# A gated-convolution and gMLP decoder with grouped experts on one core: the beginning of the expert stages, four more early loads, and stationary tiles of 128 columns

## The reference

```python
x = layer_norm(ALPHA * x + mixer(x), ...)
scores = sigmoid(x @ router_w)            # 16 experts in 4 groups
# the best group by the sum of its two best, and in it the two best experts per token
gates = scores of the two, divided by their sum
for e in range(16):
    h = silu(x @ w_gate[e]) * (x @ w_up[e])      # 1024 -> 512
    y = y + gates[:, e:e+1] * (h @ w_down[e])    # 512 -> 1024
x = layer_norm(ALPHA * x + y, ...)
```

## Time and profile before

| | |
|---|---|
| median of three runs | 1124.26 us |
| the profiled execution | 1123.61 us, its span 1122.0 us |
| PE busy | 1103.2 us, 98% |
| DVE busy | 827.8 us, 74% |
| ACT busy | 652.2 us, 58% |
| POOL busy | 115.2 us, 10% |
| first expert stage | from about 208 to 497 us |
| second expert stage | from about 811 to 1100 us |

### The profile page before, as it was taken

One profiled execution on the slowest core, in us unless ns is written; L12 is line 12 of the kernel. 1 busy time (PEld: TensorE's weight loads), 2 busy tenths in 40 slices (PEclk: granted clock), 3 DMA queues, 4 the chain that ended last, 5 costly groups with the idle time before them and its releaser, 6 DMA issues.

```text
span 1122.0 us, 15395 instructions
## 1 busy us (share of the span) xinstructions
PE 1103.2 (98%) x5448; PEld 872.4 (78%) x5448; DVE 827.8 (74%) x1023; ACT 652.2 (58%) x761; POOL 115.2 (10%) x104
## 2 busy tenths in 40 slices
PE   9999999899999999999999999999999999999996
PEld 8888888577777777777888888888757777777774
DVE  4554546899888989989516545535699898988996
ACT  4422323588887888854417332213558788887873
POOL 2000000031111111021000000000004111111113
PEclk9999999999999999999999999999999999999999
DMA  9925421699999999988304222340389999999986
GB/s 333 401 80 222 150 94 40 224 394 392 390 374 394 385 389 378 395 270 310 144 25 162 101 75 76 137 164 38 114 335 376 407 378 395 378 387 388 386 296 175
DMA packets 51752, 295.97 MB, mean 264 GB/s; under 512 B 8932, under 2 KB 9092, under 8 KB 22128
## 3 DMA queue, kind: packets, MB, share of 16 engines
q1 hardware_dynamic: 36096, 252.46, 58.1%
q0 software_dynamic: 9040, 20.91, 6.4%
q10 hardware_dynamic: 6560, 21.87, 5.1%
HBM read 277.07 MB, written 29.62 MB: 273 GB/s over the span
## 4 chain that ended last, share of the span: by engine, by line
PE 96%; DVE 2%; ACT 1%; issue 1%; DMA 0%; DVEq 0%; SPq 0%; ACTq 0%
PE ps L482 28%; PE ps L484 28%; PE ps L483 28%; PE ps L2050 2%; PE ps L1967 2%; PE ps L1892 1%; PE ps L2190 1%; PE ps L1874 1%; PE ps L1992 1%; PE ps L2090 1%; PE ps L1863 1%; PE ps L2103 0%; DMA raw<-in_w_dense 0%; DVE lo L478 0%; PE ps L1915 0%
## 5 line engine op out<-in xcount | busy, mean ns | idle before, releaser
L478 DVE TENSOR_TENSOR lo<-raw,hi 128x1024 fp32r<-128x1024 f32 x320 | 376.8, 1220 | 87.8 <-ACT hi L467 86.7
L467 ACT ACTIVATE hi<-raw 128x1024 fp32r<-128x1024 f32 x320 | 323.5, 1056 | 116.2 <-PE ps L484 80.2
L482 PE MATMUL ps<-hi,xgT_hi 128*112 128x512 f32 x480 | 190.3, 396 | 0.0
L484 PE MATMUL ps<-hi,xgT_lo 128*112 128x512 f32 x480 | 188.7, 393 | 0.0
L483 PE MATMUL ps<-lo,xgT_hi 128*112 128x512 f32 x480 | 187.5, 391 | 0.0
L478 DVE TENSOR_TENSOR lo<-raw_more,hi 128x1024 fp32r<-128x1024 f32 x128 | 153.5, 1222 | 30.1 <-ACT hi L467 27.9
L467 ACT ACTIVATE hi<-raw_more 128x1024 fp32r<-128x1024 f32 x128 | 132.9, 1057 | 53.6 <-DMA raw_more<-in_w_moe 38.9
L482 PE MATMUL ps<-xT_hi,hi 128*128 128x512 f32 x320 | 126.5, 395 | 0.8 <-DVE lo L478 0.8
L483 PE MATMUL ps<-xT_lo,hi 128*128 128x512 f32 x320 | 124.6, 389 | 0.0
L484 PE MATMUL ps<-xT_hi,lo 128*128 128x512 f32 x320 | 124.6, 389 | 0.0
L484 PEld LDWEIGHTS ps<-hi,xgT_lo 128*112 128x112 f32 x480 | 83.8, 175 | 26.1
(11 more groups left out here) (217 smaller groups left out, 1474.8 us busy)
## 6 DMA issues: line engine op xcount, KB each, us to landing
raw<-in_w_moe SPq DMA_DIRECT2D x128, 1024.0 KB
raw_more<-in_w_moe SPq DMA_DIRECT2D x64, 1024.0 KB
raw<-in_w_dense SPq DMA_DIRECT2D x39, 1024.0 KB
y_rows<-X ACTq DMA_DIRECT2D x4, 2048.0 KB, 25.5
X<-y_rows POOLq DMA_DIRECT2D x10, 512.0 KB, 9.3
x_rows<-X ACTq DMA_DIRECT2D x8, 512.0 KB, 2.6
Y<-y_rows SPq DMA_DIRECT2D x6, 512.0 KB, 5.5
xT_raw<-in_x_t SPq DMA_DIRECT2D x4, 512.0 KB, 6.3
```

The lines of the kernel that those rows point to most:

```text
L467: nc.scalar.activation(hi[:, s, :], flat(raw_units(n)), ACT.Copy).then_inc(hi_ready, 1)
L478: eng.tensor_tensor(lo[:, s, :], flat(raw_units(n)), hi[:, s, :], ALU.subtract).then_inc(lo_ready, 1)
L482: nc.tensor.matmul(out_, a_hi, b_hi, start=first, stop=False)
L484: return nc.tensor.matmul(out_, a_lo, b_hi, start=False, stop=last)
```

## The change

It has these parts:

1. **More early loads.** Units 12 to 15 of each expert stage are loaded raw into the place in `lo` in which their own `lo` part will stand (`raw_lo`); `split_lo` then works in place. Their loads wait only for the end of the mixer's last matmuls. From unit 16 on, the 12 raw slots are used as before.
2. **Expert 0 starts on half of x0.** `first_rows` signals after its first four blocks, ACT copies them then, and `gate_up_first` waits for DVE's half only at its fifth unit.
3. **Expert 0 writes banks 2 and 3.** gate_up(1) does not wait for `hid` of expert 0 any more, turn_h(0) moves behind the first unit of gate_up(1) and `turned_hot` behind its seventh. The counts and the first row numbers now share bank 7, so `route_most` moves ahead of hidden(0) and the routing matmuls wait for it.
4. **ACT's order.** All four late splits of expert 1 stand ahead of x_hi(1). The copy to `hotT` stands in turn(0) behind its fourth split. The load of the norm's parameters `ffn_par` moves behind the loop.
5. **128 columns.** POOL zeroes columns 112 to 127 of `xgT_hi`, `xgT_lo`, `hT_hi`, `hT_lo` at the beginning of each expert stage, and the passes of `gate_up` and `down` for experts 0 to 14 take all 128 columns. `down_last` stays at 112.
6. Two semaphores are dropped and others used in their place.

```diff
+AHEAD = 4
+FIRST = len(RAW_ORDER) + AHEAD
+RAW_SLOTS = RING + MORE + AHEAD
 def raw_slot(n):
-    return slot_of(n) if layer_of(n) is None else RAW_ORDER[(n - MOE[layer_of(n)]) % len(RAW_ORDER)]
+    if layer_of(n) is None:
+        return slot_of(n)
+    j = n - MOE[layer_of(n)]
+    if len(RAW_ORDER) <= j < FIRST:
+        return RING + MORE + j - len(RAW_ORDER)
+    return RAW_ORDER[(j if j < FIRST else j - FIRST) % len(RAW_ORDER)]
...
+        raw_lo = place("raw_lo", [P, RING, UN], F32)
+        lo = nc.alloc_sbuf_tensor_at("lo", [P, RING, UN], F32R, offset=top[0] - RING * UN * 4)
...
-                if raw_slot(n) >= RING and n - MOE[layer_of(n)] < len(RAW_ORDER):
+                if raw_slot(n) >= RING and n - MOE[layer_of(n)] < FIRST:
                     sp.wait_ge(unit_used, MOE[layer_of(n)])
... POOL, experts
+                for side in (xgT_hi, xgT_lo, hT_hi, hT_lo):
+                    chain.post(nc.gpsimd.memset(side[:, :, T:P].bitcast(F32), 0.0))
                 chain.step(nc.gpsimd.tensor_copy(ident_b[layer][:, :], ident[:, :]))
... ACT, turn
                     for k in range(GU - 1):
+                        if is_zero(e) and k == DN:
+                            act.wait_ge(hotT_in, layer + 1)
+                            copy(hotT[layer][0:T, :, :], ps[0:T, 2:4, :]).then_inc(hotT_ready, 1)
                         if n0 + k not in WHOLE:
                             split_hi(act, n0 + k, step, i)
                     silu(e + 1, step, i)
-                    if is_zero(e):
-                        act.wait_ge(hotT_in, layer + 1)
-                        copy(hotT[layer][0:T, :, :], ps[0:T, 2:4, :]).then_inc(hotT_ready, 1)
... ACT, experts
-                act.wait_ge(xgT_ready, m0 + 1)
+                act.wait_ge(x0_half, layer + 1)
                 copy(x0[:, 0:4, 0:T], slots(ps[:, 5:6, :])).then_inc(xgT_hi_ready, 1)
                 preload(ACT.Silu)
+                act.wait_ge(xgT_ready, m0 + 1)
...
+                for k in range(4, GU):
+                    split_hi(act, gu0(layer, 1) + k)
                 x_hi(1)
                 silu(0)
-                split_hi(act, gu0(layer, 1) + 4)
                 h_hi(0)
-                for k in range(5, GU):
-                    split_hi(act, gu0(layer, 1) + k)
                 turn(0)
                 turn(1)
-                params(layer, 1, ffn_par[layer])
                 with act.Fori(0, 6) as i:
                     turn(2, i)
                     turn(3, i)
+                params(layer, 1, ffn_par[layer])
... DVE, experts
                 x_lo(1)
+                route_most(layer)
                 hidden(0)
... PE, gate_up and down
-                    if c + m0:
+                    if c != 1:
                         pe.wait_ge(hid_ready, plus(c + m0, i))
...
-                            ins = passes(ps[0:T, h, :], xgT_hi[:, k, 0:T], xgT_lo[:, k, 0:T], hi[:, s, cols], lo[:, s, cols],
+                            ins = passes(ps[:, h, :], xgT_hi[:, k, :], xgT_lo[:, k, :], hi[:, s, cols], lo[:, s, cols],
...
-                            ins = passes(ps[0:T, 2 + h, :], hT_hi[:, k, 0:T], hT_lo[:, k, 0:T], hi[:, s, cols], lo[:, s, cols],
+                            ins = passes(ps[:, 2 + h, :], hT_hi[:, k, :], hT_lo[:, k, :], hi[:, s, cols], lo[:, s, cols],
... PE, gate_up_first and what follows it
-                    pe.wait_ge(xgT_lo_ready, m0 + 1)
...
                     for k in range(GU - 2):
+                        if k == GU // 2:
+                            pe.wait_ge(xgT_lo_ready, m0 + 1)
...
+                def beside_first(k):
+                    if k % 2:
+                        gates_to_slots(layer, (k - 1) // 2)
+                    elif k == 0:
+                        turn_h(0)
+                    elif k == GU - 2:
+                        turned_hot()
+
                 gate_up_first()
-                turn_h(0)
-                gate_up(1, between=lambda k: gates_to_slots(layer, (k - 1) // 2) if k % 2 else None)
-                turned_hot()
+                gate_up(1, between=beside_first)
                 turn_x(2)
```

More of the change, by code:

```diff
@@ L115, in pair_count @@
 def pair_count():
-    seen, out = [0] * ((RING + MORE) // 2), []
+    seen, out = [0] * (RAW_SLOTS // 2), []
     for n in range(0, UNITS, 2):
@@ L190, in hybrid_decoder @@
         hi = place("hi", [P, RING, UN], F32R)
-        lo = place("lo", [P, RING, UN], F32R)
+        raw_lo = place("raw_lo", [P, RING, UN], F32)
+        lo = nc.alloc_sbuf_tensor_at("lo", [P, RING, UN], F32R, offset=top[0] - RING * UN * 4)
         zone = top[0]
@@ L341, in sem @@
             return ctx.enter_context(nc.semaphore(name))
-        raw_in = [sem(f"raw_in{s}") for s in range((RING + MORE) // 2)]
+        raw_in = [sem(f"raw_in{s}") for s in range(RAW_SLOTS // 2)]
         unit0_in = sem("unit0_in")
@@ L358, in hybrid_decoder @@
         xt_lo = sem("xt_lo")
-        ws_masked = sem("ws_masked")
         ws_tr = sem("ws_tr")
@@ L393, in hybrid_decoder @@
         xg_in = [sem(f"xg_in{b}") for b in range(2)]
+        x0_half = sem("x0_half")
         xgT_ready = sem("xgT_ready")
@@ L421, in hybrid_decoder @@
         first_in = [sem(f"first_in{t}") for t in range(NT)]
-        tile1_in = [sem(f"tile1_in{k}") for k in range(2)]
+        tile1_in = xt_in[0:2]
         second_in = [sem(f"second_in{t}") for t in range(NT)]
@@ L452, in raw_units @@
                 return raw[:, s:s + count, :]
+            if s >= RING + MORE:
+                s = slot_of(n)
+                return raw_lo[:, s:s + count, :]
             return raw_more[layer_of(n)][:, s - RING:s - RING + count, :]
@@ L490, in hybrid_decoder @@
         LGB = (4, 2)
-        CNT = 2
-        IDA = (7, 3)
+        IDA = 7
+        CNT = 7
         NA = 3
@@ L922, in _ @@
             nc.gpsimd.affine_select(out=bsb[:, :, :], in_=ws_sum[:, :, :], compare_op=ALU.is_ge, fill=0.0,
-                                    base=0, pattern=[[0, H], [-1, P]], channel_multiplier=1).then_inc(ws_masked, 1)
+                                    base=0, pattern=[[0, H], [-1, P]], channel_multiplier=1).then_inc(consts, 1)
             def fetch(layer, c, i=0):
@@ L970, in experts @@
                         wait_lo(pool, V0 + 1)
-                        pool.wait_ge(tile1_in[0], 16)
+                        pool.wait_ge(tile1_in[0], 16 * 2)
                         chain.step(nc.gpsimd.tensor_tensor(X[:, 1, :], X[:, 1, :], Y[0][0][1][:, :], ALU.add))
-                        pool.wait_ge(tile1_in[1], 16)
+                        pool.wait_ge(tile1_in[1], 16 * 2)
                         pool.wait_ge(tile1_go, 1)
@@ L1103, in silu @@
                         act.wait_ge(hid_ready, plus(c + m0, i))
-                    nc.scalar.activation(sgate[0:T, :], ps[0:T, 0, :], ACT.Silu).then_inc(silu_ready, 1)
+                    bank = 2 if is_zero(c) else 0
+                    nc.scalar.activation(sgate[0:T, :], ps[0:T, bank, :], ACT.Silu).then_inc(silu_ready, 1)
                 def h_hi(c, i=0, dst=hT_hi):
@@ L1458, in route_ids @@
             def route_ids(layer):
-                es, bank = slice(0, NA), IDA[layer]
+                es, bank = slice(0, NA), IDA
                 dve.wait_ge(ids_ready, layer + 1)
@@ L1532, in hidden @@
                         dve.wait_ge(hT_ready, plus(c + m0, i))
-                    nc.vector.tensor_tensor(hid[0:T, :], sgate[0:T, :], ps[0:T, 1, :], ALU.mult).then_inc(hid_ready, 1)
+                    bank = 3 if is_zero(c) else 1
+                    nc.vector.tensor_tensor(hid[0:T, :], sgate[0:T, :], ps[0:T, bank, :], ALU.mult).then_inc(hid_ready, 1)
                 def h_lo(c, i=0, parts=(hT_hi, hT_lo)):
@@ L1591, in experts @@
                     own_lo(gu0(layer, 1) + k)
-                route_most(layer)
                 turn(0, gates=True)
@@ L1779, in _ @@
             conv_tile(0)
-            pe.wait_ge(consts, 1)
-            pe.wait_ge(ws_masked, 1)
+            pe.wait_ge(consts, 3)
             for h in range(H):
@@ L1894, in first_rows @@
                                            skip_group_check=True)
+                    if t == NT - 1 and k == KD // 2 - 1:
+                        ins.then_inc(x0_half, 1)
                 if t == NT - 1:
@@ L1900, in first_ids @@
                 pe.wait_ge(hot_ready, 2 * NT * layer + t + 1)
-                ins = sum_by_slot(hot[layer][t], IDA[layer], t, 0, 3, range(NA))
+                ins = sum_by_slot(hot[layer][t], IDA, t, 0, 3, range(NA))
                 if t == NT - 1:
@@ L1923, in gates_to_slots @@
                     pe.wait_ge(gates_done, layer + 1)
+                    pe.wait_ge(most_ready, layer + 1)
                 pe.wait_ge(hot_ready, 2 * NT * layer + NT + t + 1)
@@ L2029, in turned_hot @@
                     pe.wait_ge(idx_ready, 2 * layer + 1)
-                    pe.wait_ge(most_ready, layer + 1)
                     for q in range(2):
@@ L2046, in gate_up_first @@
                     pe.wait_ge(xgT_hi_ready, m0 + 1)
```

(5 more changed lines are left out.)

## The result

The changed kernel is slower: median 1127.98 us (1124.92 to 1129.57, 8 runs) against 1125.01 us for the kernel before (1123.64 to 1125.84, 8 runs), ratio 1.0027, 95% interval 1.0018 to 1.0036. The forecast was 1118.0. The execution that the profile shows took 1124.92 us (span 1123.3), the shortest of the eight.

The account below looks back on a forecast made before the run. PE bounds the kernel (96% of the chain), with DMA nearly full. Stage beginnings 2.9 plus width 2.9 make 5.8 us off 1123.61, giving 1117.8, or 1118.5 as median; predicted 1118.0, range 1115.0 to 1121.8.

Parts of the forecast that it names:

- Part 2: Stage beginning on PE: the 1.36 us wait for x0 goes; expert 0's products end at 222.0 instead of 223.36.
- Part 3: Stage beginning, other banks: gate_up(1) starts at 222.65 instead of 224.58, 1.93 us earlier, including a new 0.65 us wait.
- Part 1, the early loads: Weight queue at stage start: units 12 to 15 issued before 210 us; the lead does not add up over the stage.
- Part 5, the width: Matmuls of experts 0 to 14: 128 columns cut steps from 228.75 to 226.7 ns, worth 2.9 us, bounds 0 and 4.5.
- Part 4, the copy ahead of three splits: ACT's queue, expert 1: hidden(1) at 240.45 instead of 239.17, PE waits 0.4 us, gate_up(2) at 244.0 instead of 245.43.
- Part 1, the reserve: Weight lead at expert 14: 1.3 us before, stays at 1.5 to 2 us after the change, so PE does not starve.
- rival D: ACT's queue behind the hotT wait: reload chain slips, every later landing 3 us late, 1127 us; chance 0.05.
- Rival B: Expert stages: loads hold PE back, only 1.3 us earlier at expert 14 instead of 2.7; 1121 us, chance 0.11.
- `ffn_par` behind the loop: Stage end: the later 1 MB load falls where weight loads run out; taken as nothing, +1 us as upper bound.

Follow-up runs that it names:

- e15: The changed kernel with only the hotT copy back behind silu(1) on ACT, ffn_par still behind the loop: 1121.80 us, ratio 0.9974.
- e12: The changed kernel with the ffn_par loads ahead of turn(0) and the hotT copy back behind silu(1): 1119.42 us, ratio 0.9957.
- e1: The changed kernel with the ffn_par loads back between turn(1) and the loop, nothing else: 1127.20 us, ratio 1.0026.
- e5: The changed kernel with silu of expert 15 ahead of the split of unit 190 on ACT: 1129.89 us, ratio 1.0043.
- e16: The changed kernel with silu(15) on ACT and hidden(15) on DVE both ahead of unit 190's split: 1133.43 us, ratio 1.0083.
- e20: The changed kernel with silu(15) and hidden(15) ahead of unit 190's split, run once more with a profile: 1139.15 us.

## Why the prediction was wrong

**Part 2 and Part 3, the beginning.** Right in size and place: gate_up(1), hidden(1) and gate_up(2) within 0.1 us, 1.37 us gained in layer 0 where 1.45 were forecast.

**Part 1, the early loads.** They cost something that I had not seen. DMA is busy 0.75 from 200 to 212 us and not 0.34, the rows that POOL waits for are written later, and its first gather starts at 211.61 and not 208.83. PE turns the gathered rows at 217.52 without a wait, so this is covered. And the pause in the issues behind the early loads leaves the stream idle in part, 0.49 busy from 229 to 234 us even in e15 (1.01 before).

**Part 5, the width.** The mechanism was right and the size too large: 17.60 us an expert and not the 17.55 forecast, 1.6 us in the run and not 2.9. A run of 48 passes gained 0.057 us and not 0.08, a run of 24 nothing and not 0.03 (averages over experts 3 to 13 of layer 0). The full steps came as forecast, 226.6 against 228.9 ns, but the first ten or so of every run are slower than with 112 columns, the very first by 11 to 13 ns (314.9 against 301.9 in gate_up). I had taken the short runs of a dense stage for those of the experts. Why a run begins more slowly with 128 columns is not shown. A weight load of 128 columns takes 188 ns in the changed kernel too. The rows print these loads as f32, so the prediction had no ground to read a shorter load out of a rule for inputs that are not FP32; the sum took nothing from it. The memsets took 0.71 us together and cost nothing.

**Part 4, the copy ahead of three splits. The step that failed.** The sum priced it on the path alone: hidden(1) 1.3 us later, a wait of 0.4 us. But the three splits also free the slots of units 20 to 22, and so issue the next loads. The slip that this makes was at nothing in the sum and in the reserve of Part 1; it stood in the prediction's rival D, with a chance of 0.05, the right place (ACT's queue behind the `hotT` wait) and nearly the right time (1127). What it measured: the lead at expert 2 is 2.6 us and not 4.5, and undoing the copy's place and nothing else (e15) brings 6 us back. Rival D's own account was too strong in size. It had every later landing 3 us late; hidden(2) is 0.45 us later than before, and hidden(13) of layer 0 is 1.9 us earlier.

**Part 1, the reserve.** I had 1.3 us at expert 14 from the earlier trace rows, took away 2.7 for the faster PE, added 2.6 for `ffn_par` and 0.5 for the early pairs, and concluded that PE does not starve. In the profiled execution x_lo(14) is ready 1.2 us ahead of gate_up(14) in layer 0 (454.11 against 455.31) and not at all in layer 1 (1057.08 against 1057.21). The credit for `ffn_par` did come: against the kernel before, `hid` goes from 0.45 us late at expert 2 of layer 0 to 1.9 us early at expert 13, 2.3 us. It was a loan, though. The reserve was worked out up to expert 14 only, and the 1 MB came back behind it. "`ffn_par` has left" and "2.6 us of DMA time are freed" were also the reasons to hold rivals B and D small. Rival B, a PE held back by its loads, came true in kind, but in this execution only by tenths of a microsecond ahead of expert 14; its cap of 1121 took no account of the stage's end.

**`ffn_par` behind the loop.** Priced at nothing, with +1 us as the bound. It cost about 2 us with the lead in order (e15 against e12), because 1 MB among the last pairs is late exactly where silu(15) stands behind a split. I had not looked at what stands behind the last splits. The fall of the clock after the idle time of 2.56 us added 1.6 us.

Together: with both orders put right the kernel takes 0.9957 of the time before, which on 1124.26 us is 1119.4 and not the 1118.0 forecast, and the width's missing 1.3 us is nearly all of the rest.

How the loss divides over the eight runs of the changed kernel is not shown, nor why they reach from 1124.9 to 1129.6: its two profiles are of runs near 1125. In e1 (profiled at 1127.2) the additional time lay in waits for x_lo, in e5 (1130.7) in such waits, in those before turn_h(15) and in the slow clock behind the first of them. That the same holds for the changed kernel's slower runs is argued from them.

## What to carry to other kernels

Where DMA and an engine are both near full, find the lead of the stream at each step of the stage, up to the last one, and treat it as a budget: a faster engine spends it, and so does an edit that frees a buffer later, even if the edit is hidden on every engine. Price a moved instruction by the loads that it releases. Put bytes that may come at any time where the stream's queue is empty. To see whether the stream is a kernel's limit, time a version of both kernels that loads less: if only one of them gains, the stream limits that one. And when a rival of your own names the place of a failure, ask what its "against" rests on: here it rested on bytes that had only been put off.

## What the runs showed that was not expected

The rate of a full stream differs between stages of the same program: 387 and 383 GB/s in the two layers of the second profile of the kernel before (387 and 387 in the first), at a DMA share of 0.99 to 1.00. One per cent of it is 2 us in a stage, as much as the lead of the changed kernel at expert 13 of layer 0.

PE probably stood still for its instructions. In e16 and e20 5.1 to 5.5 us of idle time marked issue precede a step of the last sums, the instruction packet that otherwise came ahead of the sums came 5 to 7 us after they had begun, and each time PE went on 2.4 to 2.5 us after it. It shows in three stage ends of four of this kernel and in no other profile. That the packet held PE is inferred from these times, and what delays it is not shown.
